# Two raw buffers for the norms of the second attention, its projections dealt earlier, its outputs split pair by pair, in a two-layer streaming encoder step

## What is computed

```python
def trunk_layer(x, ...):
    h = rms_norm(x, norm1)
    a_q, a_k, a_v, b_q, b_k, b_v, i_q, i_k, i_w = split_cols(h @ w_in, PROJ_SPLITS)
    b_q = rms_norm(b_q.reshape(B, T, N_HEADS_B, HEAD_DIM), q_norm)
    b_k = rms_norm(b_k.reshape(B, T, N_HEADS_B, HEAD_DIM), k_norm)
    ...
    o_a = stick_breaking(a_q, ka, va, q_pos, k_pos)                        # 8 heads of 64
    o_b = indexed_sparse_attention(b_q, kb, vb, i_q, ki, i_w, ...)         # 8 heads of 64
    x = x + jnp.concatenate([o_a, o_b], axis=-1) @ w_out
    f, conv_new = conv_ffn(rms_norm(x, norm2), ...)
    return x + f, new_rows + (conv_new,)
```

## Time and profile before

| | |
|---|---|
| median of 3 runs | 1693.79 us (1690.46 to 1697.04) |
| the profiled execution | 1691.3 us, of which 1689.5 us are the span of the trace |
| granted TensorE clock, mean over the span | 0.979 of full |
| PE busy | 1591.6 us (94%) |
| PEld busy | 1471.0 us (87%) |
| DVE, ACT, POOL busy | 966.1, 683.6, 631.2 us |
| share of PE in the chain of work that ended last | 72%, DVE 14%, ACT 6% |
| first layer: b_phase from BL(0) to BL(16) | 281.45 to 392.46 us |
| second layer: the same | 1108.59 to 1214.82 us |

### The profile page before, as it was taken

The page is one execution under the profiler, slowest core; times in us unless marked ns, Lnnn a source line. Parts: engine busy times, 40 slices in busy tenths (PEclk is TensorE's granted clock), DMA queues, the critical chain, the costliest instruction groups (busy, mean ns, idle before and its releaser), DMA issues.

```text
span 1689.5 us, 29872 instructions
## 1 busy us (share of the span) xinstructions
PE 1591.6 (94%) x11754; PEld 1471.0 (87%) x11762; DVE 966.1 (57%) x1764; ACT 683.6 (40%) x1296; POOL 631.2 (37%) x346
## 2 busy tenths in 40 slices
PE   6999998888999999999999999978899999999998
PEld 5788886766999999999987888766699999999998
DVE  6657666753666336616767667657365661663461
ACT  4335453543344224314433354534434431442342
POOL 5223331322733433433552333222255343334332
PEclk9999998988999999999999999999999999999999
DMA  6322210111333332233233222111123223323233
...
DMA packets 242178, 131.43 MB, mean 78 GB/s; under 512 B 10302, under 2 KB 236590, under 8 KB 242038
## 3 DMA queue, kind: packets, MB, share of 16 engines
...
## 4 chain that ended last, share of the span: by engine, by line
PE 72%; DVE 14%; ACT 6%; issue 3%; DVEq 3%; POOL 2%; ACTq 1%; DMA 0%; SPq 0%
PE g_ps L1168 13%; PE g_ps L1169 13%; PE g_ps L1172 13%; PE a_ps L1169 7%; PE a_ps L1172 7%; PE a_ps L1168 7%; PE a_ps L1261 2%; PE a_ps L1247 1%; POOL w_lo L1687 1%; DVE score L734 1%; PE a_ps L688 1%; DVE a_ps L1663 1%; ACT work L977 1%; DVE top L731 1%; DVE va L1481 1%
## 5 line engine op out<-in xcount | busy, mean ns | idle before, releaser
L1687 POOL TENSOR_TENSOR w_lo<-raw,w_hi 128x1024 fp32r<-128x1024 f32 (+2 forms) x210 | 504.6, 2403 | 710.7 <-ACT w_hi L884 710.7
L1168 PE MATMUL g_ps<-h_hi,w_hi 128*128 128x272 f32 (+1 forms) x1616 | 453.1, 298 | 14.7 <-DVEq L1570 8.8
L1169 PE MATMUL g_ps<-h_lo,w_hi 128*128 128x272 f32 (+1 forms) x1616 | 441.6, 292 | 0.0
L884 ACT ACTIVATE w_hi<-raw 128x1024 fp32r<-128x1024 f32 (+2 forms) x210 | 217.3, 1035 | 452.3 <-PE g_ps L1172 315.6
L1172 PE MATMUL g_ps<-h_hi,w_lo 128*128 128x272 f32 (+1 forms) x1616 | 338.6, 291 | 0.0
L1168 PEld LDWEIGHTS g_ps<-h_hi,w_hi 128*128 128x128 f32 (+1 forms) x1616 | 308.5, 191 | 28.8 <-DVEq L1570 10.7
L1169 PEld LDWEIGHTS g_ps<-h_lo,w_hi 128*128 128x128 f32 (+1 forms) x1616 | 308.4, 191 | 1.2 <-issue 0.5
L1579 DVE SCALAR_TENSOR_TENSOR wts<-work,par,wts 128x546 f32<-128x546 f32 x176 | 201.0, 1142 | 99.2 <-ACT wts L1061 92.1
L1172 PEld LDWEIGHTS g_ps<-h_hi,w_lo 128*128 128x128 f32 (+1 forms) x1616 | 255.9, 190 | 0.0
L1168 PE MATMUL a_ps<-h_hi,w_hi 128*128 128x272 f32 x720 | 194.4, 288 | 0.0
L1169 PE MATMUL a_ps<-h_lo,w_hi 128*128 128x272 f32 x720 | 194.3, 289 | 0.0
...
## 6 DMA issues: line engine op xcount, KB each, us to landing
...
```

Source lines behind the costliest of these rows:

```text
L884: act.activation(w_hi[:, n % SPLIT, 0:kt, 0:c], raw[:, n % RAW, 0:kt, 0:c], ACT.Copy).then_inc(hi_done, 1)
L1168: pe.matmul(g[0:c, a, 0:HALF], w_hi[:, s, j, 0:c], xh[:, mov], start=(j == 0), stop=False)
L1169: pe.matmul(g[0:c, a, 0:HALF], w_hi[:, s, j, 0:c], xl[:, mov], start=False, stop=False)
L1687: pool.tensor_tensor(w_lo[:, s, 0:kt, 0:c], raw[:, n % RAW, 0:kt, 0:c], w_hi[:, s, 0:kt, 0:c].bitcast(F32), ALU.subtract).then_inc(lo_done, 1)
```

## The change

- A second buffer for raw queries and keys. Queries keep nraw, keys take the last eighth of o_t, which lies idle until the last pair's output (norm_raw).
- The projections are dealt anew. In a_phase G(bq, 0) takes the place of G(bv, 2), and all of bq 0, bk 0, bq 1, bk 1 and the first half of bq 2 are made before BL(0). In b_phase the norm of the keys of pair p + 1 and of the queries of pair p + 2 lie a step or more ahead of their use, in the even steps 0 to 8. Steps 7, 10, 13, 14 and 16 hold no half; before it was 0, 10, 14 and 16. The second half of the fill, G(wo, 1, 0), stands behind the last product.
- E, which stood in odd steps beside steps with M, now stands in the same even step as N, Y and M, behind M. W of the queries goes to the end of the next odd step.
- The copies to q_smp go from DVE (in W) to ACT, as steps QS.
- O(4) to O(7) follow their pairs (steps 5, 9, 13 and the end) and take the 512 prompt columns; a new step OS takes the 32 sample columns of all four at once, behind the last product. Their parts lie where keys and values of the sample cache of the first attention lay (o_high_k, o_high_a).

```diff
-    fill = [("aq", 1), ("ak", 1), ("aq", 2), ("ak", 2), ("aq", 3), ("ak", 3), ("bv", 0), ("bv", 1), ("bv", 2)]
+    fill = [("aq", 1), ("ak", 1), ("aq", 2), ("ak", 2), ("aq", 3), ("ak", 3), ("bv", 0), ("bv", 1), ("bq", 0)]
...
+    s += [("AS", 7), ("AX", 7), ("N", "bk", 0), ("Y", "bk", 0), bk1[0], ("M", "bk", 0), ("W", "bk", 0), ("TOPK", 1), ("ASZ",), ("AW", 3)]
+    s += [("N", "bq", 1), bk1[1], ("ASP",), ("Y", "bq", 1), ("E", "bk", 1), ("S", "bk", 1), ("ASS",), ("M", "bq", 1), ("W", "bq", 1), bq2[0], ("ASV",)]
...
+    def norm(j, *unit):
+        return [("N", *unit), ("BR", j), ("Y", *unit), ("M", *unit)]
...
+    first[0] = norm(0, "bk", 1)
+    half[0] = [bq2[1], ("E", "bq", 2)]
+    after[0] = [("W", "bk", 1), ("S", "bq", 2)]
+    first[1] = [("T", "bk", 0), ("BR", 1)]
+    half[1] = [bk2[0]]
+    first[2] = norm(2, "bq", 2)
+    half[2] = [bk2[1], ("E", "bk", 2)]
+    after[2] = [("S", "bk", 2)]
+    first[3] = [("T", "bk", 1), ("BR", 3)]
+    half[3] = [bq3[0]]
+    after[3] = [("W", "bq", 2)]
...
+        def norm_raw(kind):
+            return nraw[:] if kind == "bq" else o_t[:, KT - 1, :]
...
+                elif k == "OS":
+                    act.wait_ge(o_out.sem, o_out.at(l, ("b", "s")))
+                    act.wait_ge(v_out.sem, v_out.at(l, "b"))
+                    act.activation(o_high_a[:, :, SEQ:TOK], o_t[:, PAIRS:PAIRS + 2, SEQ:TOK], ACT.Copy)
+                    act.activation(o_high_k[:, :, SEQ:TOK], o_t[:, PAIRS + 2:KT, SEQ:TOK], ACT.Copy).then_inc(o_hi.sem, 1)
...
-                        dve.tensor_tensor(halves(nraw[:]), g, halves(rstd[:]), ALU.mult)
+                        dve.tensor_tensor(halves(norm_raw(kind)), g, halves(rstd[:]), ALU.mult)
```

More of the change, by code:

```diff
@@ L168, in b_phase @@
     first, half, after = ({j: [] for j in range(n + 1)} for _ in range(3))
[L169 to L192, removed]
-    for j in range(last, n):
-        first[j] += [("BR", j)]
+    def norm(j, *unit):
+        return [("N", *unit), ("BR", j), ("Y", *unit), ("M", *unit)]
+    bq2, bk2, bq3, bk3 = (product(kind, p) for p in (2, 3) for kind in ("bq", "bk"))
@@ new lines, in b_phase @@
+    bv2, bv3 = (product("bv", p) for p in (2, 3))
+    first[0] = norm(0, "bk", 1)
[9 more added lines that the diff above has]
+    after[3] = [("W", "bq", 2)]
+    first[4] = norm(4, "bk", 2)
+    half[4] = [bq3[1], ("E", "bq", 3)]
@@ new lines, in b_phase @@
+    after[4] = [("W", "bk", 2), ("S", "bq", 3)]
+    first[5] = [("BR", 5)]
+    half[5] = [bk3[0]]
+    first[6] = norm(6, "bq", 3)
+    half[6] = [bk3[1], ("E", "bk", 3)]
+    after[6] = [("S", "bk", 3)]
+    first[7] = [("T", "bk", 2), ("BR", 7)]
+    after[7] = [("W", "bq", 3)]
+    first[8] = norm(8, "bk", 3)
+    half[8] = [bv2[0]]
+    after[8] = [("W", "bk", 3)]
+    first[9] = [("T", "bk", 3), ("BR", 9)]
+    half[9] = [bv2[1], ("E", "bv", 2)]
+    first[10] = [("T", "bv", 2), ("BR", 10)]
@@ L195, in b_phase @@
+    first[11] = [("BR", 11)]
+    half[11] = [bv3[0]]
+    first[12] = [("BR", 12)]
+    half[12] = [bv3[1], ("E", "bv", 3)]
+    first[13] = [("T", "bv", 3), ("BR", 13)]
+    for j in range(14, n):
+        first[j] = [("BR", j)]
+    half[15] = [("G", "wo", 0, 0)]
+    half[n] = [("O", KT - 1)]
+    for p, j in enumerate((0, 1, 3, 7)):
+        after[j] += [("QS", p)]
     for j in range(9):
@@ L198, in b_phase @@
         after[9 + j // 2] += [("O", j)]
+    for p in range(PAIRS - 1):
+        after[QB * p + 5] += [("O", PAIRS + p)]
     s = []
@@ L202, in b_phase @@
             s += [("BL", j), ("BX", 2 * j), ("BX", 2 * j + 1)]
-        s += first[j] + half[j]
+        s += first[j] + (half[j] if j < n else [])
         if j >= 2 and B_TILES[2 * j - 4][1] == QB - 1:
@@ L208, in b_phase @@
         s += after[j]
-    s += [("BV", "s")]
+    s += half[n] + [("BV", "s"), ("OS",), ("G", "wo", 1, 0)]
     return s
@@ L232, in layer_steps @@
     s += b_phase()
-    s += [("O", j) for j in range(KT // 2, KT)]
     s += [("G", "wo", 0, 1), ("E", "wo", 0), ("X", 2, 0), ("G", "wo", 1, 1), ("E", "wo", 1), ("X", 2, 1)]
@@ L491, in trunk @@
         bt_out = ev("bt_out", btiles)
-        o_hi = ev("o_hi", list(range(KT)))
-        o_split = ev("o_split", list(range(KT)))
+        o_order = {l: [st[1] if st[0] == "O" else "s" for at, st in steps if at == l and st[0] in ("O", "OS")] for l in range(DEPTH)}
+        o_hi = ev("o_hi", o_order)
+        o_split = ev("o_split", o_order)
         c_tap = ev("c_tap", [(n, f) for f in range(FT) for n in ("ua", "ug")])
@@ L665, in o_high, with o_cols @@
         def o_high(j):
-            return act_lo[:, (j + KT // 2) % KT, :]
+            if j < PAIRS:
+                return act_lo[:, j + PAIRS, :]
+            return (o_high_a, o_high_k)[(j - PAIRS) // 2][:, j % 2, :]
+        def o_cols(j):
+            return slice(0, TOK if j < PAIRS else SEQ)
         def f_place(f):
@@ L910, in _ @@
                         act.wait_ge(r_full.sem, r_full.at(l, ("R", 1)))
-                    act.activation(sq_slot(st), nraw[:], ACT.Square).then_inc(sq_done.sem, 1)
+                    act.activation(sq_slot(st), norm_raw(st[1]), ACT.Square).then_inc(sq_done.sem, 1)
                 elif k == "Y":
```

47 lines of the change are left out of this document (27 added, 20 removed).

## The result

The changed kernel takes 1697.5 us (median of 17 runs, 1693.4 to 1703.3) against 1693.2 us (17 runs, 1690.5 to 1697.0): ratio 1.0024, interval 1.0015 to 1.0033. A second series gave 1.0014 (1.0002 to 1.0026). It is slower, as forecast, but by 4 us instead of 9, and that lies within the 0.5% that I had counted as no change; over 17 executions each the interval leaves out 1. The span of the profiled execution grew from 1689.5 to 1694.7 us, PE's busy time by 8 us; the granted clock fell from 0.979 to 0.973.

A forecast was written before the change was run, and what follows sets the result against it. It took DVE's chain to bound b_phase; +0.6 (steps at full clock), +9 (clock), -1.5 (ahead of BL(0)) and +1.5 (behind the last product) give +9.6 on 1691.3, 1700.9; the runs' median, 2.5 higher, 1703. Range 1682 to 1714.

The forecast's parts named there:

- DVE's chain: In b_phase DVE's sequence of operations sets the step times; two steps cost it 13.6 us in place of 14.3.
- The collision: Steps 0, 2, 4, 6: POOL's w_lo falls on DVE's M and holds its third operation, 2.2 us each time.
- The steps: b_phase lengths from BL to BL at full clock: -2.1 and +2.7 us in the two layers, together +0.6.
- The clock: b_phase: PE's waits over 2 us before a half lower its clock; 4.5 us a layer, +9 (0 to 1.5 each).
- rival (a): b_phase: w_lo misses M in the even steps, so the lock-out does not take place; -8, 1685 us; chance 0.25.
- Ahead of BL(0): Stretch before b_phase: BL(0) 3.2 and 2.0 us earlier, less 1.8 each for a slow stretch; -1.5 together (-5 to +2).
- The wait at ASS: Before BL(0): ASS, which waited 0.85 us, waits some 3.6, as M and W of keys 0 precede ASZ on DVE.
- Behind the last product: After b_phase: G(wo, 1, 0) covers the 2.16 us wait but its 3.2 come back; +1.5 together (0 to +3).
- The two ends: Stretches before BL(0) and after the last product: -1.5 and +1.5 us.
- (b): b_phase: w_lo holds M but PE's clock stays up; +0.6, 1694 us; chance 0.2.
- (c): b_phase: the clock falls behind every wait, six at 1.5 us a layer; +18 in place of +9, 1712; chance 0.15.
- my own sum: Whole kernel, the author's own case: w_lo holds M and the clock dips half the time; +9.6, 1703 us; chance 0.4.

The follow-up runs named there:

- both repairs: The change with C of steps 0, 2, 4, 6 moved to the next odd step and the pre-BL(0) top-k round behind W of queries 1: 1670.0 us (0.9845).

## Why the prediction was right or wrong

**DVE's chain is the bound: right for the change, not without limit.** Freeing PE of every wait for E gained nothing, with the collision or without it. Raising PE's clock in b_phase gained nothing. The collision, 2 us of DVE at a time, was worth 14 us out of the change and 17.6 into the kernel before. But ahead of BL(0) and in steps 10 to 15 a slow stretch of PE did cost time, and with both repairs in, 7.1 us less work of DVE a layer gave 4.0 and 2.2.

**The collision: right in place, mechanism and nearly in size.** I took 2.2 us in eight steps, 17.6 us. It came in full five times (2.0 over the 0.73) and at 0.9 in the other three; it was worth 14 us. By the rule of the Trainium skill that I had named (SBUF — State Buffer, Who interferes with whom) the one that issues first keeps the pair. The rows agree: M issued 0.16 us behind w_lo took 2.76; in step 4, where M's third operation was in flight as w_lo began, M kept its 0.73 and w_lo took 2.61. E, which reads one of its inputs from PSUM, ran in 0.72 in the middle of that w_lo. Where w_lo began during M's second operation (step 6 of both layers) both paid: w_lo took 2.73 and M's third operation 2.70. How little decides was right too: in step 0 w_lo began 0.16 us ahead of M's third operation, in step 4 0.35 behind it. I had not seen that both would occur in one run.

**The steps.** Forecast at the full clock and measured (first and second layer): steps 0 and 1 14.4, measured 16.3 and 13.1; 2 and 3 15.4, 17.4 and 17.3; 4 and 5 16.5, 13.1 and 13.5; 6 and 7 16.1, 15.8 and 15.5; 8 and 9 15.6, 15.5 and 15.5; 10 to 15 30.9, 32.4 and 32.4. The sum over both layers was forecast at 217.8 at the full clock and came out at 217.9, with the dips in it. That agreement is luck: its terms are off by -3.4 to +2.0 us. Steps 1, 3, 11 and 15 had dips that the 217.8 leaves out, and steps 4 and 5 (and 0 and 1 of the second layer) went without the collision that it counts.

**The clock: this is the step that failed.** I set 4.5 us a layer, +9, on top of those sums; b_phase came out 0.6 us longer than before, not 9.6. The dips were there, even outside the bound of 1.5 that I gave each: 2.1 us in each of the halves of steps 1 and 3 in the first layer. They did cost time where they stood: steps 2 and 3 take 17.4 us with one and 14.8 without, and steps 10 to 15 were 2.3 us a layer shorter at the full clock. What failed is that I added them to the collision as if the two did not touch. A slow half in step 3 makes w_hi and w_lo of step 4 late enough to miss M, and DVE, which my chain had 1.7 us behind BL(4), waits for PE there instead: steps 4 and 5 take 13.1 to 13.5 us in place of 18.3 to 18.7. That is more than the dip costs. I had written under rival (a) that "a low clock in step 0 or 2 is enough for M", and yet added both; the slow halves that decided stood in the odd steps. With PE kept busy (granted clock 0.92 and 1.00 in the two windows of the first layer, 0.91 and 0.89 beside it), the collision came back into step 4 and the sum stayed at 217.6. That both ways come to nearly the same sum is measured, not derived. One reading was wrong as well: the wait of 1.90 ahead of BL(15) was followed by a dip in the first layer of the kernel before (its half took 4.8 us at a clock of 0.67), and only in the second by none (3.35).

**Ahead of BL(0): wrong in sign.** Forecast -1.5, measured +1.8. The wait at ASS was near (3.6 forecast, 2.84 and 3.21 measured), its cause was not: I put it down to M and W of the keys 0, and with them still in place it went with the top-k round. Mis-sized was the slow stretch behind it, "as the old one did, 1.8 each": ASS lost 2.8 (6.4 for 3.6) and the half behind it 1.4 (4.70 for 3.3), 4.2 in place of the 1.8. And I had not asked what else stood in DVE's queue ahead of ASZ: that round was worth 14 us. Nor had I seen that w_lo meets M here too: the first operation of M of the queries 1 takes 1.70 us in both layers, and it does so in every run of the change, so no experiment says what that costs.

**Behind the last product: right in kind.** Forecast +1.5 with bounds 0 and +3, measured +2.8. Undoing it costs 4 us.

**The sum.** The two ends were forecast at 0 together and cost 4.6, b_phase was forecast at +9.6 and cost 0.6. The errors partly cancel, so that the total of 4 us lies nearer to the forecast 9 than its largest term does.

**The rivals.** (a) without the collision was put at 1685; with C moved it gave 1682.9. (b), collision and full clock, at 1694, gave 1697.7 where most of the low clock in b_phase was taken away; it took the ends at nothing, which cost 4.6 in the change. (c), the clock falling behind every wait, was near to what PE did, and far from what the time did. With the clock's 9 us left out, my own sum is 1694, and with the measured ends 1699, against 1697.5.
